# Expert layers of a decoder trunk: slots of 128 tokens with one expert each, or of 32 tokens with four experts each

## The chip, the cores and the metric

The kernel runs on one core of one Trainium2 chip. The metric is the device time of one execution, in microseconds; a lower one is better. The time before is the median of three runs.

## What is computed

One inference step of a two-layer decoder trunk for 512 new prompt tokens and 8 sample tokens, all in float32, model width 1024. The even layer has a convolution and a gated linear attention branch, the odd layer latent attention. Each of the two is followed by an expert layer, and that is what the change touches:

```python
def peer(h, w_q, sub_keys, u_tab, v_tab):   # 8 heads, 16 experts of 16384 per head and token
    q = (xf @ w_q).reshape(n, H_P, 2, D_HALF)
    s = jnp.einsum('nhcd,hckd->nhck', q, sub_keys)
    s_top, i_top = lax.top_k(s, TOPK)
    cand = s_top[:, :, 0, :, None] + s_top[:, :, 1, None, :]
    c_top, c_idx = lax.top_k(cand.reshape(n, H_P, TOPK * TOPK), TOPK)
    ids = i1 * N_KEYS + i2                  # i1, i2: looked up in i_top by c_idx
    gates = jax.nn.softmax(c_top, axis=-1)
    act = jax.nn.gelu(jnp.einsum('td,thkd->thk', xb, u_tab[ids])) * gates
    return jnp.einsum('thk,thkd->td', act, v_tab[ids])
```

For each token and head, 16 experts are chosen. An expert is one row of u and one row of v, 4 KB each. The token's normalised x is dotted with u, the result goes through gelu and is multiplied with the gate, and v is summed with that weight over heads and experts.

## The kernel before, in words

`program` (at the end of the file) runs the even layer, `peer_layer` 0, the odd layer and `peer_layer` 1, each behind a barrier of all engines. Layer 1 also applies the final norm and writes the result.

In `peer_layer` the 512 prompt tokens are four tiles (NT) of 128 tokens, one token per partition. A tile has 8 heads, so there are NW = 32 heads in order, numbered n, and each has 16 **slots**. Slot k of a head is one indirect DMA of POOL (L1096): for each of the 128 tokens, the row of u and v of its k-th expert, 8 KB, into one of RING = 8 buffers `rows`. The 8 sample tokens have 8 slots more, ahead of head 24, in which the 128 partitions already hold 16 picks of each token. A layer has 520 slots.

The order of the work is written out by hand, engine by engine, with semaphores:

- **POOL** issues gather after gather. It waits for `rows_used`, which PE raises when the slot eight places earlier is used up, and at a head's start for its ids (`routed`). For the first head of a layer it waits only for the first 8 ids (`routed_early`).
- **DVE** waits for a landed slot and forms the dot product of all 128 rows with `x_n` (L1414, `dot`). Between the dots it routes the head two places on (AHEAD = 2): `first8`, `next8`, `pairs`, `lookup` and `softmax` at the groups 3 to 7 of a head (a group is two slots). It also normalises the next tile's x (L1280) and adds the finished sum of a tile to x (`add_to_x`, L1423), in one operation of 128x1024.
- **ACT** makes of a slot's 128 dots the weights (`weigh`): gelu (L1178), product with the gate (L1180), and the identity scaled by it, 128x128 (`diag`, L1184). It also copies the queries, their transposes and the scores out of PSUM, computes the exponentials (`exps`, L1170) and the mean squares (`mean_square`, L1121).
- **PE** multiplies the 128x128 `diag` of a slot with its 1024 columns of v, in two matmuls of 512 columns (`experts`, L1581), and sums into one of two accumulators of two PSUM banks over the 128 slots of a tile. At the start of a head stand the `queries` of the head two places on (L1531), behind the first group their transposes (L1545), behind the second the `scores` (L1559). In heads 5, 13 and 21 (TILE_ENDS) the next tile's x is transposed behind the third group (L1508). In heads 16 to 20 the sample's norm, transposes, spread (L1521), queries in column groups of 32 (L1539), scores and routing are done.
- **SP** loads, at a layer's start, the norm's gain, the query weights of 8 heads (1 MB each), the keys (1 MB) and four small constants; in layer 1 also the final norm's gain.

A layer begins with norm, transposes, queries, scores and routing of heads 0 and 1; the first gather follows as soon as head 0's first 8 ids are there.

## Time and profile before

| what | value |
|---|---|
| median of 3 runs | 3477.43 us (3475.92 to 3477.55) |
| the profiled execution's own time, first to last instruction | 3501.1 us |
| PE busy (matmuls) | 2983.7 us, 85% |
| DVE busy | 2185.4 us, 62% |
| ACT busy | 1438.0 us, 41% |
| POOL busy | 1301.9 us, 37% |
| gathered and loaded by POOL's queue | 1128.34 MB, 77.8% of 16 engines' span |
| first and last issue of a gather by ids | 322.7 and 3471.9 us |

A busy time is the time in which an engine had an instruction in work; matmuls are pipelined, so a busy PE is not PE at its peak. The slices are fortieths of the span (87.5 us each). In the timeline a row gives start, duration, engine, line, operation, what is written from what, the form, how many, and in brackets the idle time before and what ended it. The expert layers run from about 300 to 1643 us and from 2150 us to the end.

### The profile page before, as it was taken

The numbers are of one execution on the slowest core, as the hardware profiler recorded it, in microseconds if no ns is written. First come the engines' busy times: TensorE is split into PE (matmuls) and PEld (weight loads), VectorE is DVE, ScalarE is ACT, GpSimd is POOL, SyncE is SP. The second block draws the span as 40 slices with busy tenths as digits, with TensorE's granted clock in tenths as the row PEclk, the third lists the DMA queues.
The fourth block names the chain that finished last, engine by engine and source line by source line (L and its number), as shares of the span: only waits on it lengthen the run. The fifth ranks groups of instructions, "written<-read, shape, count | busy, mean of one in ns | idle before, by whom it ended". The sixth has DMA issues, their size and how long they took to land. (4 is left out here: it accounts for less than half of the span.)

```text
span 3501.1 us, 34014 instructions
## 1 busy us (share of the span) xinstructions
PE 2983.7 (85%) x10561; PEld 1480.5 (42%) x10561; DVE 2185.4 (62%) x5266; ACT 1438.0 (41%) x4182; POOL 1301.9 (37%) x1112
## 2 busy tenths in 40 slices
PE   8987888888889888887999886888888888888886
PEld 7653333433334433333554764434333434433332
DVE  4874667666667766664362334666766676766765
ACT  3122445444444544443351222444444444544444
POOL 0211444444544444452001010445444454444442
PEclk9988999999999999999999897999999999999999
DMA  4015999999999999998203345999999999999998
GB/s 163 29 52 228 421 421 414 421 421 415 420 398 421 418 421 421 421 419 350 81 1 162 134 165 220 421 421 414 421 421 421 415 408 421 409 421 421 421 419 355
DMA packets 178372, 1194.53 MB, mean 341 GB/s; under 512 B 22320, under 2 KB 28240, under 8 KB 38150
## 3 DMA queue, kind: packets, MB, share of 16 engines
q0 software_dynamic: 154368, 1128.34, 77.8%
q1 hardware_dynamic: 22525, 63.11, 4.8%
q8 instruction: 84, 1.38, 0.2%
q10 hardware_dynamic: 1296, 0.90, 0.1%
q14 instruction: 99, 0.80, 0.1%
HBM read 1188.29 MB, written 4.46 MB: 341 GB/s over the span
## 5 line engine op out<-in xcount | busy, mean ns | idle before, releaser
L1581 PE MATMUL p_acc<-p_rows,p_diag 128*128 128x512 f32 (+1 forms) x4160 | 1973.0, 616 | 412.8 <-ACT p_diag L1184 411.0
L1414 DVE CUSTOM_DVE_ANT_0 p_rows<-p_rows,p_x_n 128x1024 f32<-128x1024 f32 x1024 | 1243.7, 1223 | 790.5 <-DMA p_rows<-in_peer_uv,p_ids 788.4
L1096 POOL DMA_INDIRECT p_rows<-in_peer_uv,p_ids x1024 | 1217.0, 1188 | 1384.6 <-PE p_acc L1581 1281.6
L1581 PEld LDWEIGHTS p_acc<-p_rows,p_diag 128*128 128x128 f32 (+1 forms) x4160 | 752.9, 192 | 1508.5 <-ACT p_diag L1184 790.8
L1178 ACT ACTIVATE p_acts<-p_dots 128x1 f32<-128x1 f32 x1040 | 208.3, 200 | 871.8 <-DVE p_dots L1414 870.4
L1184 ACT ACTIVATE p_diag<-ident,p_gated 128x128 f32<-128x128 f32 x1024 | 410.9, 401 | 33.6
L1180 ACT ACTIVATE p_gated<-p_acts,p_gates 128x1 f32<-128x1 f32 x1024 | 301.6, 295 | 33.2
L1531 PE MATMUL p_q_bank<-p_w_q,p_xT 128*128 128x256 f32 x1024 | 234.9, 383 | 2.2 <-ACT p_xT L1127 2.2
L1531 PEld LDWEIGHTS p_q_bank<-p_w_q,p_xT 128*128 128x128 f32 x1024 | 196.1, 192 | 55.5 <-issue 28.5
L1150 ACT COPY p_q_rows<-p_q_bank 128x256 f32<-128x256 f32 x68 | 25.2, 370 | 347.7 <-PE p_q_bank L1531 347.7
L1623 POOL DMA_INDIRECT smp_past<-in_cache_rows,smp_row_ids x32 | 30.0, 937 | 361.1 <-PE c_ps L2096 227.4
L1178 ACT ACT_TABLE_LOAD x73 | 93.7, 1283 | 8.7 <-DVE p_dots L1414 7.5
L2469 PE MATMUL d_turn<-ident,smp_past 128*128 128x128 f32 x512 | 78.0, 311 | 15.6 <-DVE d_kpeT L2353 14.4
L541 DVE SCALAR_TENSOR_TENSOR a_conv<-a_u,a_conv_wc,a_conv 128x512 f32<-128x512 f32 x120 | 86.6, 792 | 0.0
L688 PE MATMUL a_ps<-a_xT,a_w_in 128*128 128x260 f32 x384 | 85.7, 384 | 0.1
L1414 DVE DVE_READ_ACCUMULATOR2_ANT p_dots<- 128x1 f32 x1040 | 85.1, 82 | 0.0
L1170 ACT ACT_TABLE_LOAD x64 | 82.1, 1283 | 1.1
L688 PEld LDWEIGHTS a_ps<-a_xT,a_w_in 128*128 128x128 f32 x384 | 72.5, 190 | 11.9 <-issue 0.4
L2469 PEld LDWEIGHTS d_turn<-ident,smp_past 128*128 128x128 f32 x512 | 68.8, 162 | 19.9 <-DVE d_kpeT L2353 16.3
L2359 DVE COPY d_ckvT<-d_turn 128x512 f32<-128x512 f32 x64 | 42.1, 687 | 56.2 <-PE d_turn L2469 56.1
L2294 ACT COPY d_ckvT<-d_turn 128x512 f32<-128x512 f32 x64 | 34.7, 587 | 103.0 <-PE d_turn L2469 103.0
L1088 POOL MEMSET p_eps<- 128x1 f32 x2 | 0.2, 98 | 171.2 <-POOLq L62 171.2
(402 smaller groups left out, 2483.0 us busy)
## 6 DMA issues: line engine op xcount, KB each, us to landing
p_w_q<-in_w_q_heads SPq DMA_DIRECT2D x16, 1024.0 KB, 12.2
p_rows<-in_peer_uv,p_ids POOLq DMA_INDIRECT x1024
a_w_in<-in_ab_w_in SPq DMA_DIRECT2D x6, 1024.0 KB
a_w_in<-in_ab_w_out SPq DMA_DIRECT2D x1, 4096.0 KB
c_arena<-in_c_w_out SPq DMA_DIRECT2D x1, 4096.0 KB, 12.7
smp_past<-in_c_w_out SPq DMA_DIRECT2D x1, 4096.0 KB
a_w_in<-in_ab_w_in SPq DMA_DIRECT2D x4, 1008.0 KB, 21.3
smp_past<-in_w_qx SPq DMA_DIRECT2D x1, 3072.0 KB, 18.6
```

What stands on the lines that cost most here:

```text
L541: ins = nc.vector.scalar_tensor_tensor(out=conv[:, c, 0:SEQ], in0=u[:, c, i:i + SEQ], scalar=conv_wc[:, c, i:i + 1], in1=conv[:, c, 0:SEQ] ...
L688: last = nc.tensor.matmul(ps[bank][:, 512 * b:512 * b + half], w_in[:, k, at:at + 128], xT[:, k, half_of(b)], start=(k == 0), stop=(k == K ...
L1096: nc.gpsimd.indirect_dma_start(out=rows[:, slot % RING, :], out_offset=None, in_=w[f"peer_uv{layer}"], in_offset=bass.IndirectOffsetOnAxis ...
L1170: nc.scalar.activation(ex[:], rel[:], ACT.Exp, accum_out=ex_sum[:]).then_inc(ex_ready, 1)
L1178: nc.scalar.activation(acts[:, i % 4, j:j + 1], dots[:, i % 4, j:j + 1], ACT.Gelu).then_inc(gelud, 1)
L1180: nc.scalar.mul(gated[:, i % 4, j:j + 1], acts[:, i % 4, j:j + 1], gate[:, j:j + 1]).then_inc(gated_ready, 1)
L1184: nc.scalar.mul(diag[:, i % 4, j, 0:n], unit[:], gated[:, i % 4, j:j + 1]).then_inc(diag_ready, 1)
L1414: nc.vector.tensor_tensor_reduce(rows[:, k % RING, 0:D_MODEL], rows[:, k % RING, 0:D_MODEL], x, 1.0, 0.0, ALU.mult, ALU.add, dots[:, slot ...
L1531: last = nc.tensor.matmul(q_bank[:, 0:D_KEY], xT[:, k, :], w_q[:, h, k, :], start=(k == 0), stop=(k == KC - 1))
L1581: last = nc.tensor.matmul(acc[done % 2][0:n, at], diag[:, slot // GROUP % 4, j, 0:n], rows[:, (slot + j) % RING, D_MODEL + 512 * b:D_MODEL ...
L2359: nc.vector.tensor_copy(buf(g)[:, half, :], bank(0, half)).then_inc(turn_dve, 1)
L2469: last = nc.tensor.transpose(turn[i % 2][:, KEYS * c + 128 * a:KEYS * c + 128 * a + 128], latent(b, NQ * g + a, c), ident[:])
```

## The change

A slot now holds four experts of each of 32 tokens, for the same 128 tokens and experts in all. The tile's tokens are four quarters q ("quads"), and the 16 slots of a head are four for each q. On partition 32 e + p of a slot sits token 32 q + p with its experts of index e modulo 4.

- ids and gates are computed as before, with a token per partition, into `pick`. Then PE moves them into the new arrangement with 16 small matmuls (`spread_picks`, 32 identity columns and 8 columns of data each), and DVE copies them from PSUM into `ids` and `gates`, in two operations. POOL and ACT wait for that (`picked`). In the loop it stands behind the first group on PE and the third on DVE, for the head after the present one.
- x is repeated four times: for each q, two matmuls of 512 columns (`spread_x`) write the 32 tokens' rows into all four quarters of the partitions, and ACT copies them out (`x_rep_out`, 128x1024). For the first tile this stands among the steps of the start, for the others in the last head of the tile before. DVE's dots use this copy.
- the weights are 128x32 (32 identity columns) in place of 128x128. The sum runs in four column groups: 256 of the 1024 columns each, into 32 partitions each of one of four accumulators (one per q, a half bank each), which take two banks in all.
- adding the sum to x is now 8 operations of 32x256 for two of the quarters, twice a tile; for the sample 4 of 8x256.
- the first head's early ids are gone: the first gather waits for all of them and for the moved picks.
- one more constant of 64 KB is loaded; in layer 1 the final gain is loaded later, into the buffer of the norm's gain, once all norms are done. PSUM for transposes is shared in one counted order of turns.

```diff
...
-                if n == 0:
-                    pool.wait_ge(routed_early, 1)
-                else:
-                    pool.wait_ge(routed, route_no(n) + 1)
+                pool.wait_ge(picked, n + 1)
...
+            def x_rep_out(t, q):
+
+                act.wait_ge(turn_ps, rep_turn(t, q) + 1)
+                if t:
+                    act.wait_ge(dotted, first_slot(H_P * t - 1) + QUADS * (q + 1))
+                nc.scalar.copy(x_rep[:, q, :], turn[:, :]).then_inc(turn_used, 1)
...
-                    nc.scalar.mul(diag[:, i % 4, j, 0:n], unit[:], gated[:, i % 4, j:j + 1]).then_inc(diag_ready, 1)
+                    nc.scalar.mul(weights[:, i % 4, j, 0:n], unit, gated[:, i % 4, j:j + 1]).then_inc(weights_ready, 1)
...
             s_out(0)
+            x_rep_out(0, 0)
+            x_rep_out(0, 1)
             q_out(1)
             qT_out(1, qT[:])
+            x_rep_out(0, 2)
             exps(0)
             s_out(1)
+            x_rep_out(0, 3)
             exps(1)
...
+            def spread_picks(m):
+
+                dve.wait_ge(pick_ps, m + 1)
+                nc.vector.tensor_copy(ids[:, m % (AHEAD + 1), :].rearrange("p (q j) -> p q j", q=QUADS), by_quad[:, :, 0, :])
+                nc.vector.tensor_copy(gates[:, m % (AHEAD + 1), :].rearrange("p (q j) -> p q j", q=QUADS), by_quad[:, :, 1, :]).then_inc(picked, 1)
...
+            def add_to_x(t, bank):
+
+                for q in (2 * bank, 2 * bank + 1):
+                    dve.wait_ge(rows_used, first_slot(H_P * t + H_P - 1) + QUADS * (2 * bank + 2))
+                    for c in range(PARTS):
+                        at = x_sb[quad(q), t, part(c)]
+                        last = nc.vector.tensor_tensor(at, at, acc[quad(c), q, :], ALU.add)
+                last.then_inc(acc_used, 1)
...
+            def spread_x(t, q):
+
+                if t == 0 and q == 0:
+                    pe.wait_ge(small_in, 80)
+                pe.wait_ge(turn_used, rep_turn(t, q))
+                for b in range(2):
+                    at = slice(512 * b, 512 * b + 512)
+                    last = nc.tensor.matmul(turn[:, at], quads[quad(q), :], x_n[quad(q), at], start=True, stop=True)
+                last.then_inc(turn_ps, 1)
...
+            def spread_picks(m):
+
+                pe.wait_ge(routed, route_no(m) + 1)
+                pe.wait_ge(gates_ready, route_no(m) + 1)
+                if m:
+                    pe.wait_ge(picked, m)
+                for q in range(QUADS):
+                    for e in range(4):
+                        last = nc.tensor.matmul(by_quad[quad(e), q], ident[:, quad(q)], pick[:, :, e:TOPK:4], start=True, stop=True)
+                last.then_inc(pick_ps, 1)
...
-                    pe.wait_ge(diag_ready, slot + j + 1)
-                    for b in range(2):
-                        at = slice(512 * b, 512 * b + 512)
-                        last = nc.tensor.matmul(acc[done % 2][0:n, at], diag[:, slot // GROUP % 4, j, 0:n], rows[:, (slot + j) % RING, D_MODEL + 512 * b:D_MODEL + 512 * b + 512],
+                    pe.wait_ge(weights_ready, slot + j + 1)
+                    for c in range(PARTS):
+                        at = D_MODEL + D_PART * c
+                        last = nc.tensor.matmul(dst[QUAD * c:QUAD * c + n], weights[:, slot // GROUP % 4, j, 0:n], rows[:, (slot + j) % RING, at:at + D_PART],
                                                 start=(first and j == 0), stop=(end and j == GROUP - 1))
                     last.then_inc(rows_used, 1)
...
                 scores(m)
+                spread_x(0, 2 * m)
+                spread_x(0, 2 * m + 1)
+            spread_picks(0)
+            spread_picks(1)
...
+                    if g % 2 and h == H_P - 1 and t < NT - 1:
+                        spread_x(t + 1, q)
```

## Rows read from the trace of the kernel before

**Rows 1.** The page: GB/s moved by the DMA engines in 40 equal slices.

```profile
GB/s 163 29 52 228 421 421 414 421 421 415 420 398 421 418 421 421 421 419 350 81 1 162 134 165 220 421 421 414 421 421 421 415 408 421 409 421 421 421 419 355
```

**Rows 2.** Waits of POOL: for whom; us in total, times, longest us.

```profile
POOL p_rows L1096 <- PE p_acc L1581: 1302.9, 903, 10.4
```

**Rows 3.** Groups by line: busy us, mean ns of one; idle before, releasers.

```profile
L1581 PE MATMUL p_acc<-p_rows,p_diag 128*128 128x512 f32 (+1 forms) x4160 | 1973.0, 616 | 412.8 <-ACT p_diag L1184 411.0
L1414 DVE CUSTOM_DVE_ANT_0 p_rows<-p_rows,p_x_n 128x1024 f32<-128x1024 f32 x1024 | 1243.7, 1223 | 790.5 <-DMA p_rows<-in_peer_uv,p_ids 788.4
...
L1178 ACT ACTIVATE p_acts<-p_dots 128x1 f32<-128x1 f32 x1040 | 208.3, 200 | 871.8 <-DVE p_dots L1414 870.4
L1184 ACT ACTIVATE p_diag<-ident,p_gated 128x128 f32<-128x128 f32 x1024 | 410.9, 401 | 33.6
L1180 ACT ACTIVATE p_gated<-p_acts,p_gates 128x1 f32<-128x1 f32 x1024 | 301.6, 295 | 33.2
...
L1309 DVE TENSOR_TENSOR p_cand<-p_top 128x256 f32<-128x256 f32 x66 | 27.6, 419 | 0.0
```

**Rows 4.** Windows of 40 us: busy by engine, then granted clock, DMA share, GB/s.

```profile
410.00:450.00 40.00, 33.10 (x86) 14.94 (x84) 26.84 (x66) 17.58 (x54) 18.66 (x17) 1.00 1.01 421
530.00:570.00 40.00, 34.96 (x94) 16.99 (x94) 28.34 (x71) 22.17 (x61) 20.26 (x17) 0.96 0.99 406
970.00:1010.00 40.00, 35.25 (x90) 16.67 (x88) 27.56 (x66) 19.94 (x60) 17.28 (x15) 0.87 0.93 369
2820.00:2860.00 40.00, 34.14 (x93) 16.27 (x93) 29.07 (x71) 21.21 (x63) 21.63 (x16) 0.96 0.96 393
```

**Rows 5.** Windows at the start of layer 0, columns as in rows 4.

```profile
300.00:324.00 24.00, 15.28 (x64) 12.21 (x65) 8.57 (x38) 6.78 (x12) 1.42 (x2) 0.79 0.97 385
312.00:316.00 4.00, 2.98 (x16) 2.19 (x16) 0.00 (x0) 0.74 (x2) 0.00 (x0) 1.00 1.01 424
```

**Rows 6.** Timeline of the start of layer 0.

```profile
315.37 0.68 PE L1559 MATMUL p_s_bank<-p_keysT,p_qT 128*128 128x128 f32 x4 [0.55 <-ACT p_qT L1154]
315.89 3.62 PE L1531 MATMUL p_q_bank<-p_w_q,p_xT 128*128 128x256 f32 x16
...
319.37 0.43 DVE L1313 MAX8 p_best<-p_cand 128x8 f32<-128x256 f32 x1
...
320.96 0.68 PE L1559 MATMUL p_s_bank<-p_keysT,p_qT 128*128 128x128 f32 x4 [0.56 <-ACT p_qT L1154]
...
322.68 1.14 POOL L1096 DMA_INDIRECT p_rows<-in_peer_uv,p_ids  x1 [22.41 <-DVE p_ids L1343]
```

**Rows 7.** Timeline: the sample's spread of x and its queries in column groups.

```profile
1035.23 1.98 PE L1521 MATMUL p_turn<-p_x_smp,p_spread 8*128 8x512 f32 x4
...
1037.25 1.01 ACT L1146 COPY p_x_smp<-p_turn 128x1024 f32<-128x1024 f32 x1 [0.28 <-PE p_turn L1521]
...
1075.61 3.66 PE L1539 MATMUL p_q_bank<-p_w_q,p_xT_smp 128*32 128x256 f32 x64
1079.20 6.28 PE L1581 MATMUL p_acc<-p_rows,p_diag 128*128 128x512 f32 x14
```

**Rows 8.** Chain of waits at the start of layer 1: start us, us, what.

```profile
2149.97 4.19 DMA p_gain<-in_ffn_norm
```

**Rows 9.** Timeline, POOL and PE, at the starts of heads 3, 5 and 16 of layer 0.

```profile
458.58 3.70 PE L1581 MATMUL p_acc<-p_rows,p_diag 128*128 128x512 f32 x8 [1.33 <-ACT p_diag L1184]
...
460.83 0.94 POOL L1096 DMA_INDIRECT p_rows<-in_peer_uv,p_ids  x1 [5.11 <-PE p_acc L1581]
...
540.27 5.40 PE L1581 MATMUL p_acc<-p_rows,p_diag 128*128 128x512 f32 x8 [2.74 <-ACT p_diag L1184]
...
544.14 1.83 POOL L1096 DMA_INDIRECT p_rows<-in_peer_uv,p_ids  x1 [8.12 <-PE p_acc L1581]
...
985.04 5.46 PE L1581 MATMUL p_acc<-p_rows,p_diag 128*128 128x512 f32 x6 [2.83 <-ACT p_diag L1184]
```

**Rows 10.** Timeline behind the last gather of layer 1.

```profile
3491.60 1.22 DVE L1423 TENSOR_TENSOR x_sb<-x_sb,p_acc 128x1024 f32<-128x1024 f32 x1 [1.89 <-PE p_acc L1581]
```

More of the change, by code:

```diff
@@ L1141, in smp_xT_out @@
                         at = DEC_BATCH * u + 16 * twin
-                        nc.scalar.copy(xT_smp[:, u, :, at:at + DEC_BATCH], src).then_inc(smp_xT, 1)
+                        nc.scalar.copy(xT_smp[:, u, :, at:at + DEC_BATCH], src).then_inc(turn_used if u and twin else smp_xT, 1)
             def smp_spread_out():
-                act.wait_ge(smp_spread, 1)
-                nc.scalar.copy(x_smp[:], turn[:, :]).then_inc(smp_full, 1)
+                act.wait_ge(turn_ps, SMP_REP_TURN + 1)
+                nc.scalar.copy(x_smp[:], turn[:, :]).then_inc(turn_used, 1)
             def q_out(i):
@@ L1490, in _ @@
                         if g == 6 + late:
-                            lookup(route_no(m), ids[:, m % (AHEAD + 1), :])
+                            lookup(route_no(m), pick[:, 0, :], m)
                 if m < NW:
-                    softmax(route_no(m), gates[:, m % (AHEAD + 1), :])
-            add_to_x(4, NT - 1)
+                    softmax(route_no(m), pick[:, 1, :])
+            add_to_x(NT - 1, 1)
             if out:
@@ L1534, in smp_queries @@
             def smp_queries(u):
-                pe.wait_ge(smp_xT, 4)
+                pe.wait_ge(smp_xT, 3)
+                pe.wait_ge(turn_used, SMP_X_TURN + 1)
                 pe.wait_ge(qT_ready, smp_query_no(u))
+                for j in range(4):
+                    pe.wait_ge(w_q_in[4 * u + j], 16)
                 for k in range(KC):
```

211 lines of the change are left out of this document (104 added, 107 removed).

## The prediction

> **What bounds the kernel now.** First the page's slices: in both expert stages the DMA engines move 414 to 421 GB/s nearly throughout, and the few lower slices (408, 409, 398) are what a change there could win back [rows 1]. A gather brings 128 rows of 8 KB, 1.0486 MB, so at 421 GB/s a slot takes 2.49 us, and 1040 slots take 2590 us of the span of 3501.1. Then the waits: POOL waits 1302.9 us for PE, since a slot of the ring must be free [rows 2], and DVE's idle time before its dots, 788.4 us, ends with a landed gather [rows 3]. Both belong to one loop: eight slots go round gather, dot, gelu and weights, expert matmuls. Which part limits it is read from the groups: per slot, DVE needs 1.22 us, ACT 0.90 (0.20 + 0.30 + 0.40), and PE four instructions (4160 for 1040 slots) whose starts lie some 0.44 us apart, as eight take 3.70 and one 0.6, so some 1.75 us [rows 3, 9]; each is under 2.49. PE looks 85% busy, yet the DMA engines are what is full. The windows confirm it: a common 40 us stretch moves 421 GB/s at DMA share 1.01, and only a few move less: 406, 369, 393 [rows 4].
>
> So the matmuls that the change makes cheaper are covered by the gathers. The time can move in three places only: where the DMA engines run dry, before the first gather of a layer, and behind the last one.
>
> **The gathers themselves: 0.** A slot still has 128 rows of 8 KB, and there are still 1040. Plain weight loads run at much the same rate (424 in the window 312 to 316, before any gather [rows 5]), so it is the engines that limit, not which rows are asked for. The 512 KB for the final gain move from the start of layer 1 into its gathers, where they cost 1.2 us that the start saves.
>
> **The expert matmuls: off the path.** A slot becomes four column groups of 256 columns, eight instructions (each float32 call shows as two). The nearest row is the sample's queries, 128x32 weights and 256 columns in four groups: 64 in 3.66 us, 0.057 us each [rows 7]; eight are 0.46 us, where 1.75 stood. If groups did not overlap, 16 query matmuls in 3.62 us (0.226 each) give 1.8 us, no change [rows 6]. I take 0.5. Of ACT's weights, 0.40 goes towards 0.30; hidden too.
>
> Switching between whole-width and 32-column matmuls costs nothing visible: those 64 begin at 1075.61, take 3.66 and are followed by expert matmuls at 1079.20 [rows 7], no gap.
>
> **The start of a layer: the large term.** Before, the first gather is issued at 322.68, once half the ids are known [rows 6]. After, it needs all 16, the gates too, PE's spreading of both, and DVE's copy. ACT and PE also get the four repeats of x ahead of it. Step by step in layer 0, from the end of head 0's scores at 315.37 + 0.68 = 316.05: first repeat 1.98 (as the sample's spread) and its copy 1.01 [rows 7], second repeat 1.98 to 321.02; queries of head 1, 3.62, to 324.64; then from their end to the end of head 1's scores as before (319.51 to 321.64, 2.13) to 326.77 [rows 6]; third repeat 1.98 and copy 1.01 to 329.76; only then ACT's exponentials, with a table load 1.28 + 0.4, to 331.45; gates 0.5 to 331.95; 32 small matmuls at 0.057, 1.8, to 333.8; two small copies 0.4: 334.2. The Trainium skill ("TensorEngine Tiling (Array Packing)", Instruction Overhead) gives each matmul some 60 cycles of overhead and no more for few columns. By that rule, as an estimate, 32 of them take 32 x 60 cycles at 2.4 GHz = 0.8 us, and the sum at the end would be 2 us lower; no row here is that small a matmul, so I keep the nearest row's 1.8.
>
> DVE's own routing does not set the end: from its row at 319.37 [rows 6] it has eleven operations left, and even at twice 0.42 us each [rows 3] that ends at 328.6. It is the repeats ahead of the exponentials on PE and ACT that set the end. Issue is late by 11.5 us.
>
> What covers this is the load of weights. To 324 the engines had moved 385 x 24 = 9.24 MB [rows 5] of the 9.96 MB asked for before the gathers (0.52 + nine times 1.05); they run dry at 325.7. From issue to first byte no row tells directly; a 0.52 MB load took 4.19 us to landing [rows 8], 1.24 of them data, so launch and finish make 2.9; I take 2.0. Data begin at 336.2, the engines idle for 10.5 us; the twin in layer 1 makes it **+21**. Bounds: launch 0 to 3.8 (with POOL's 0.94), the small matmuls half or double: 7.5 to 14 a layer, 15 to 28 for both. Slot 8 is not late: eight gathers keep the engines fed for 20 us, to 356, and DVE's second routing (twenty-odd operations, some 9 us from 334.2), spread, first gelu and matmul end by about 351.
>
> **Where the engines ran dry.** Against 421, a stretch of 406 lacks 40 x 15/421 = 1.4 us, 369 lacks 4.9, 393 lacks 2.7 [rows 4]; one more like the last (394) lacks 2.6, three like the first (406, 405, 409) 4.0; the smaller ones 2.4: 18 us in all. They lie behind heads in which ACT does a norm and waits for queries. In a common head POOL waits 5.11 us and nothing is lost; behind a norm 8.12 us [rows 9], and PE starts at half clock there: eight instructions in 5.40 us and six in 5.46, where eight take 3.70. After: PE finishes the last two slots in 1 instead of 3.7 us, so queries begin 2.5 earlier, and the first slot frees some 3 us earlier. That would give back nearly all 18. Against it, at the turn of each tile ACT copies four repeats (1.01 each), the last one waiting for PE (1.98) between last slot and next queries: 3 to 4 us, about what was won, with more at half clock. I take **-12** (bounds -16 and, with starving turns, +4).
>
> **Inside the heads: 0.** DVE gets two small copies a head and sixteen adds of 32x256 a tile (by the 0.42 us of a 128x256 operation [rows 3], 6.7 us in place of 1.22), with 1.2 us spare per slot. PE's 32 small matmuls stand behind the head's first two slots; behind them wait transposed queries and ACT's copy, some 2 us of slack I do not see used up; DVE asks for them six slots into the head, 15 us. POOL needs the ids only ten slots later. Cover gone, 60 heads at even 0.3 us would be 18 us; it is in the upper range.
>
> **Behind the last gather.** The last slot's matmuls go from 1.9 to about 0.7 us, but eight adds stand in place of one of 1.22 us [rows 10]: 8 x 0.33 to 0.42 = 2.6 to 3.4. Net +0.3 in layer 0; in layer 1 DVE also has eight adds (2.6 to 3.4 us) inside the last head, whose final scalings leave it nearly no slack: +1.5. Together **+2** (0 to 4).
>
> **Sum:** 21 - 12 + 2 = +11. The profiled span is 3501.1, which would become 3512; the median of the runs is 3477.4, 24 us less, so I add the same 11 there: **3488 us**. Some 7 us (0.2%) is about what a measurement can tell.
>
> **Rivals.**
> 1. PE turns cold (3505, chance 0.20). With 0.5 us of work in 2.49, PE idles 2 us per slot. After 2.74 us idle, eight instructions took 5.40 us, and after 2.83 six took 5.46, where eight take 3.70 [rows 9]: half clock, 1.2 GHz. Queries would take up to 7.2 us and repeats 4.0; a tile's turn is then 16 to 18 us after its last dot where about 12 can be borne, 4 to 6 us lost at two turns a layer, 20 in all, and 2 in small dips, where 18 were lost: +4 in place of -12, so 21 + 2 + 4. For it: 2.74 us were enough. Against: 1.33 us of idle left the 3.70 untouched, and 2 us lies between. The Trainium skill ("TensorE: Matmul & The Clock Gate", HAM oscillation) says that idle gaps between bursts bring the clock back to half rate again and again. [...]
> 2. Groups don't overlap (3500, 0.07). The change does not do what it says, PE stays at 1.75 us plus new work, nothing comes back: 21 + 2. Against it stands the 0.057 us of [rows 7].
> 3. Start shorter and all stalls gone (3480, 0.15): 17 - 15 + 1 = +3, within the noise.
> 4. Faster (3470, 0.08): slots free 1.3 us earlier in each round, so more gathers queue. If that lifted 421 to 424, the rate of one window in [rows 5], 2590 x 0.7% = 18 us come off: 11 - 18 = -7. It decides from 422 on. Against: at share 1.01 the queue is full already.
> My forecast has the other 0.50.
>
> **Range.** 3478 to 3508: the unknowns of the start (15 to 28) and of the stalls (-16 to +4) partly cancel; it takes in rivals 1 to 3 and leaves out most of 4. **Chances:** faster by over 0.2%: 0.08; same: rival 3 and the low end of the forecast, 0.22; slower: 0.70.
>
> **What would show it.** First gather of layer 0 about 334 instead of 322.7, with an empty stretch of some 10 us on the DMA engines before it, in both layers: if absent, the main term is wrong. Expert matmuls 8 per slot in about 0.5 us; granted clock around the queries (1.0 or 0.5) decides between forecast and rival 1; windows of 406 and 369 back at 421, or new dips at heads 8, 16 and 24 of a layer. A common window at 424 would make rival 4 right.

## The result, and the profile after

The kernel after takes 3521.33 us (median of 4 runs, 3519.58 to 3524.04), the kernel before 3477.17 (4 runs, 3475.92 to 3477.55) on the same chip: a ratio of 1.0125 [1.0111, 1.0139], 44 us slower. The forecast was 3488 and the range ended at 3508: the direction was right, and the size was short by a factor of four.

The page after, engine line, granted clock and DMA rate in the same 40 slices as [rows 1]:

```profile
PE 2223.4 (63%) x16897; PEld 1048.8 (30%) x16897; DVE 2236.6 (64%) x5506; ACT 1380.7 (39%) x4214; POOL 1231.2 (35%) x1112
...
PEclk9988666666667666665999997666666667666665
...
GB/s 162 25 55 156 422 420 421 395 421 421 421 390 421 421 421 409 421 421 356 144 1 162 94 249 177 422 421 421 398 421 421 420 389 420 421 421 413 421 421 345
```

The full slices are as before, so a gather costs what it did. Lower are the slice in which each layer starts (228 to 156, 220 to 177) and three slices a layer (395, 390, 409, and 398, 389, 413). The granted clock lies near 0.65 in both expert layers, where it was near 1.0.

The groups by line that answer to [rows 3], and the adds and repeats:

```profile
L1626 PE MATMUL p_acc<-p_rows,p_weights 128*32 128x256 f32 x8192 | 940.1, 551 | 1172.3 <-ACT p_weights L1217 1157.4
L1217 ACT ACTIVATE p_weights<-p_quads,p_gated 128x32 f32<-128x32 f32 x1024 | 329.0, 321 | 33.5
L1541 PE MATMUL p_turn<-p_x_n,p_quads 32*128 32x512 f32 x128 | 101.7, 935 | 4.4 <-ACT p_x_rep L1160 4.4
L1439 DVE TENSOR_TENSOR x_sb<-x_sb,p_acc 32x256 f32<-32x256 f32 x128 | 53.4, 417 | 4.7 <-PE p_acc L1626 3.1
```

The matmuls did what the change meant: 940 us of PE work where 1973 stood. PE now waits 1157 us for weights, and nothing came of it.

**Three lengths locate the loss.** Each expert layer can be cut at four marks of the timeline: the load of the gain that opens it, its first gather, its last gather, and the first load of what follows (or the end of the span). Here they are for the kernel after, both layers:

```profile
301.43 0.36 SPq L1095 DMA_DIRECT2D p_gain<-in_ffn_norm  x1
...
1643.56 0.94 POOL L1127 DMA_INDIRECT p_rows<-in_peer_uv,p_ids  x1 [1.55 <-PE p_acc L1626]
...
1667.68 0.38 SPq L1773 DMA_DIRECT2D c_arena<-in_c_w_in  x1
...
2145.88 0.34 SPq L1095 DMA_DIRECT2D p_gain<-in_ffn_norm  x1
...
2185.05 0.94 POOL L1127 DMA_INDIRECT p_rows<-in_peer_uv,p_ids  x1 [38.57 <-DVE p_gates L1397]
...
3487.86 0.94 POOL L1127 DMA_INDIRECT p_rows<-in_peer_uv,p_ids  x1 [1.54 <-PE p_acc L1626]
```

With the first gather of layer 0 at 340.44 (next rows), layer 0 has a **start** of 39.0 us, a **middle** of 1303.1 and an **end** of 24.1, layer 1 has 39.2, 1302.8 and (to 3521.1) 33.2. The same cuts in every profile of this study, each as the sum of both layers:

| kernel | start | middle | end | both layers |
|---|---|---|---|---|
| before | 45.7 | 2597.6 | 51.2 | 2694.5 |
| before, second chip (e0) | 45.9 | 2597.3 | 51.2 | 2694.3 |
| **after** | **78.2** | **2605.9** | **57.4** | **2741.5** |
| after, another chip (a0) | 77.7 | 2607.0 | 57.4 | 2742.1 |
| e1 column groups alone | 48.0 | 2593.4 | 51.0 | 2692.4 |
| e2 picks first | 53.3 | 2608.7 | 57.3 | 2719.3 |
| e3 PE kept busy | 77.2 | 2629.9 | 58.3 | 2765.4 |
| e4 quarter of the adds | 79.5 | 2597.8 | 50.2 | 2727.5 |
| e6 adds later | 77.0 | 2595.1 | 59.2 | 2731.3 |
| e7 picks handed over sooner | 79.8 | 2607.6 | 57.3 | 2744.6 |
| e8 last repeat later | 77.6 | 2593.9 | 57.4 | 2728.9 |
| e9 repeats from all rows | 67.1 | 2598.7 | 57.3 | 2723.0 |
| e10 e2, e6 and e8 | 54.4 | 2595.4 | 59.1 | 2708.9 |
| e11 and weights first | 55.0 | 2593.4 | 59.2 | 2707.6 |
| e12 all moves | 54.9 | 2593.5 | 56.2 | 2704.7 |
| e13 before, weights first | 47.7 | 2595.9 | 51.1 | 2694.7 |

So the change costs 32.5 us at the starts, 8.4 in the middles and 6.2 at the ends: 47. Two kernels that share a start in their text can differ in it by some 2 us: layer 1 of e4 and e7 starts in 41.1 us, that of a0 and e6 in 38.7, though neither edit touches it. Start and middle also overlap. In before the weights are still being loaded when the first gather is issued, and the DMA engines are never empty there (share 1.00 to 1.02 in every window of 4 us from 320 to 340). In after they are empty for 14.6 us in layer 0 (windows from 324 to 348) and 14.8 in layer 1 (2168 to 2192), 29.4 together. The other 3 us of the 32.5 are load of weights that has moved out of the middle, so the stalls inside the middles grew by some 11 us and not by 8.4. A count as in the prediction says the same: over thirty-one windows of 40 us in each layer, from 10 us behind the first gather on, the rate falls short of 421 GB/s by 16.9 us of transfers in before and by 27.9 in after.

The layer between the two expert layers, which it leaves alone, takes 506.9 us in the profile of before and 478.2 in that of after; that is why the two spans differ by only 20 us, and why the sums above are compared and not the spans.

**The start of layer 0**, timeline, where [rows 6] had the first gather at 322.68:

```profile
317.87 1.98 PE L1541 MATMUL p_turn<-p_x_n,p_quads 32*128 32x512 f32 x4
...
320.95 3.78 PE L1541 MATMUL p_turn<-p_x_n,p_quads 32*128 32x512 f32 x4 [1.10 <-ACT p_x_rep L1160]
...
324.65 6.65 PE L1564 MATMUL p_q_bank<-p_w_q,p_xT 128*128 128x256 f32 x16
...
333.37 1.98 PE L1541 MATMUL p_turn<-p_x_n,p_quads 32*128 32x512 f32 x4
...
335.38 1.01 ACT L1160 COPY p_x_rep<-p_turn 128x1024 f32<-128x1024 f32 x1 [2.77 <-PE p_turn L1541]
336.41 1.28 ACT L1203 ACT_TABLE_LOAD   x1
...
339.21 0.62 PE L1617 MATMUL p_pick_bank<-p_pick,ident 128*32 128x8 f32 x32
...
340.44 1.14 POOL L1127 DMA_INDIRECT p_rows<-in_peer_uv,p_ids  x1 [38.45 <-DVE p_gates L1397]
```

The chain is the one that the prediction wrote down, down to ACT's exponentials behind the copy of the third repeat; but the second repeat and the queries run at half clock, 3.78 and 6.65 us for the 1.98 and 3.62 that were put in. What it does to the DMA engines, in windows as in [rows 5], and below them a common stretch and the first tile turn, as in [rows 4]:

```profile
320.00:324.00 4.00, 3.05 (x4) 1.16 (x4) 3.86 (x20) 0.89 (x1) 0.00 (x0) 0.55 1.01 416
...
328.00:332.00 4.00, 3.54 (x12) 2.53 (x10) 0.00 (x0) 0.37 (x1) 0.00 (x0) 0.67 0.04 16
332.00:336.00 4.00, 2.79 (x10) 1.18 (x8) 0.00 (x0) 0.99 (x2) 0.00 (x0) 1.00 0.00 0
336.00:340.00 4.00, 3.38 (x36) 1.29 (x36) 0.50 (x4) 2.92 (x6) 0.00 (x0) 0.68 0.00 0
340.00:344.00 4.00, 0.00 (x0) 0.00 (x0) 3.96 (x25) 0.33 (x1) 2.95 (x3) 0.50 0.41 125
...
410.00:450.00 40.00, 21.23 (x182) 8.60 (x182) 27.43 (x70) 16.70 (x57) 18.71 (x17) 0.63 1.01 420
...
650.00:690.00 40.00, 29.68 (x182) 12.04 (x184) 32.22 (x82) 18.25 (x57) 15.53 (x12) 0.60 0.90 368
```

Of the windows from 328 to 340 two are empty and one nearly so. The dips of [rows 4] (behind heads with a norm) are gone, and new ones stand where a tile turns, at heads 8, 16 and 24 of each layer: 368 here, then 398, 399, 368, 354 and 409 (the second of them cuts its dip in two; 975 to 1015 has 354).

**A tile turn**, timeline of PE, DVE, ACT and POOL around the first dots of head 8:

```profile
657.24 3.41 DVE L1439 TENSOR_TENSOR x_sb<-x_sb,p_acc 32x256 f32<-32x256 f32 x8
...
667.10 1.43 POOL L1127 DMA_INDIRECT p_rows<-in_peer_uv,p_ids  x1 [6.50 <-PE p_acc L1626]
...
672.34 1.22 DVE L1428 CUSTOM_DVE_ANT_0 p_rows<-p_rows,p_x_rep 128x1024 f32<-128x1024 f32 x1
...
673.44 3.78 PE L1541 MATMUL p_turn<-p_x_n,p_quads 32*128 32x512 f32 x4
...
677.15 6.19 PE L1564 MATMUL p_q_bank<-p_w_q,p_xT 128*128 128x256 f32 x16
...
683.38 0.37 ACT L1183 COPY p_q_rows<-p_q_bank 128x256 f32<-128x256 f32 x1 [5.11 <-PE p_q_bank L1564]
...
684.68 1.32 PE L1626 MATMUL p_acc<-p_rows,p_weights 128*32 128x256 f32 x16 [1.34 <-ACT p_weights L1217]
...
685.61 0.94 POOL L1127 DMA_INDIRECT p_rows<-in_peer_uv,p_ids  x1 [9.12 <-PE p_acc L1626]
```

Two delays fall close together. The eight small adds stand in the middle of DVE's routing, and POOL waits 6.50 us; then head 8's first pair of dots is done by 673.6, but ACT makes their weights only behind the copy of the queries, which wait on PE behind the last repeat: 673.44 to 683.34 for these two at half clock. No slot comes free until 685, and POOL waits 9.12.

### The profile page after: what moved, and what is told of

Same layout as the page of the kernel before. It is cut to its first block and busy times, and to the rows that moved or that the text cites. A ratio compares the mean times of both kernels' runs of the same rounds, so it can differ in the third digit from the quotient of the medians.

```text
span 3521.1 us, 47144 instructions
## 1 busy us (share of the span) xinstructions
PE 2223.4 (63%) x16897; PEld 1048.8 (30%) x16897; DVE 2236.6 (64%) x5506; ACT 1380.7 (39%) x4214; POOL 1231.2 (35%) x1112
## 5 line engine op out<-in xcount | busy, mean ns | idle before, releaser
L1428 DVE CUSTOM_DVE_ANT_0 p_rows<-p_rows,p_x_rep 128x1024 f32<-128x1024 f32 x1024 | 1242.2, 1223 | 754.7 <-DMA p_rows<-in_peer_uv,p_ids 754.5
L1626 PE MATMUL p_acc<-p_rows,p_weights 128*32 128x256 f32 x8192 | 940.1, 551 | 1172.3 <-ACT p_weights L1217 1157.4
L1127 POOL DMA_INDIRECT p_rows<-in_peer_uv,p_ids x1024 | 1146.8, 1120 | 1488.2 <-PE p_acc L1626 1273.0
L1626 PEld LDWEIGHTS p_acc<-p_rows,p_weights 128*32 128x32 f32 x8192 | 197.0, 129 | 1855.9 <-ACT p_weights L1217 1798.2
L1217 ACT ACTIVATE p_weights<-p_quads,p_gated 128x32 f32<-128x32 f32 x1024 | 329.0, 321 | 33.5
L1564 PE MATMUL p_q_bank<-p_w_q,p_xT 128*128 128x256 f32 x1024 | 334.5, 497 | 2.2 <-ACT p_xT L1153 2.2
L1213 ACT ACTIVATE p_gated<-p_acts,p_gates 128x1 f32<-128x1 f32 x1024 | 301.6, 295 | 33.2
L1564 PEld LDWEIGHTS p_q_bank<-p_w_q,p_xT 128*128 128x128 f32 x1024 | 259.2, 261 | 104.7 <-issue 52.0
L1541 PE MATMUL p_turn<-p_x_n,p_quads 32*128 32x512 f32 x128 | 101.7, 935 | 4.4 <-ACT p_x_rep L1160 4.4
L688 PEld LDWEIGHTS a_ps<-a_xT,a_w_in 128*128 128x128 f32 x384 | 72.5, 190 | 11.9 <-issue 0.4
L2524 PE MATMUL d_turn<-ident,smp_past 128*128 128x128 f32 x512 | 67.1, 284 | 0.6 <-DVE d_kpeT L2408 0.3
L2524 PEld LDWEIGHTS d_turn<-ident,smp_past 128*128 128x128 f32 x512 | 59.2, 145 | 2.9 <-DVE d_kpeT L2408 1.8
```

The lines of the kernel that those rows point to most:

```text
L688: last = nc.tensor.matmul(ps[bank][:, 512 * b:512 * b + half], w_in[:, k, at:at + 128], xT[:, k, half_of(b)], start=(k == 0), stop=(k == K ...
L1127: nc.gpsimd.indirect_dma_start(out=rows[:, slot % RING, :], out_offset=None, in_=w[f"peer_uv{layer}"], in_offset=bass.IndirectOffsetOnAxis ...
L1213: nc.scalar.mul(gated[:, i % 4, j:j + 1], acts[:, i % 4, j:j + 1], gate[:, j:j + 1]).then_inc(gated_ready, 1)
L1217: nc.scalar.mul(weights[:, i % 4, j, 0:n], unit, gated[:, i % 4, j:j + 1]).then_inc(weights_ready, 1)
L1428: nc.vector.tensor_tensor_reduce(rows[:, k % RING, 0:D_MODEL], rows[:, k % RING, 0:D_MODEL], x, 1.0, 0.0, ALU.mult, ALU.add, dots[:, slot ...
L1541: last = nc.tensor.matmul(turn[:, at], quads[quad(q), :], x_n[quad(q), at], start=True, stop=True)
```

## The experiments

Fourteen runs, two of them of kernels that are not changed, in four groups; those of one group ran on one chip, with before beside them.

**e0, before again.** No edit.

> The kernel before, unchanged, for a second profile. Its first profile had a span of 3501.1 us beside a median of 3477, and the odd layer in it took 506.9 us where the changed kernel's profile has 478.2, though nothing there was changed. If the surplus of 24 us belongs to that one execution, this profile spans about 3476 and its odd layer takes about 480 us; if profiling lengthens this kernel always, about 3501 and 507 again. Time: 3477, ratio 1.000.

3504.67 us, 0.9998 [0.9989, 1.0008]. Both expert layers take 2694.3 us, as in the profile of before to 0.2 us. On this chip and the next ones before takes 3502 to 3506 instead of 3477. The layer in between takes 503 to 510 us in their profiles, whichever kernel it is, as in the first profile of before (506.9), and 478 only in that of after. So that difference does not come from the change; whether it is the chip or the time at which it ran, no run tells.

**e1, the column groups alone.** In the kernel before, the expert matmuls take weights of 32 columns and write four column groups; the adds then take one group's columns (what is added to x is therefore wrong, and the adds are one operation still, not the eight of after).

```diff
-                    for b in range(2):
-                        last = nc.tensor.matmul(acc[done % 2][0:n, at], diag[..., 0:n], rows[..., 512 * b ...])
+                    for c in range(4):
+                        last = nc.tensor.matmul(acc[done % 2][32 * c:32 * c + m, 0:256], diag[..., 0:m], rows[..., 256 * c ...])
```

> The kernel before with the expert matmuls alone in four column groups of 32 columns of weights and 256 of data; the slots, the start, ids and adds stay as before (the sums are then not the right ones: a slot's 128 tokens share 32 output rows). Theory A, PE with little work falls to half clock: mean granted clock about 0.70 instead of 0.965, queries about 6.4 us instead of 3.6, and since neither start nor tile turns have anything added, the time stays within 3470 to 3488. Theory B, the half clock comes from something else in the change (small matmuls, waits for copies): clock 0.95 or more, stalls of the gathers nearly gone, 3477 - 15 = 3462.

3503.62 us, 0.9997 [0.9987, 1.0006]. Its expert matmuls, from the groups, and those of e3 (below), kept at full clock:

```profile
L1582 PE MATMUL p_acc<-p_rows,p_diag 128*32 128x256 f32 x8320 | 975.4, 557 | 1263.5 <-ACT p_diag L1184 1193.5
```

```profile
L1631 PE MATMUL p_acc_smp<-p_w_q,ident 128*128 128x256 f32 x5952 | 1557.9, 398 | 0.0
...
L1627 PE MATMUL p_acc<-p_rows,p_weights 128*32 128x256 f32 x8192 | 669.9, 399 | 180.8 <-ACT p_weights L1218 176.4
```

The mean granted clock falls from 0.964 to 0.702 by this edit alone, and the time does not move: neither do the cheap matmuls win much (3.9 us in the middles, of which the starts take 2.1), nor does the half clock cost anything while PE has slack. What e1 has does not cost time. What it lacks is the new work and the new order of the rows in the slots.

**e2, picks first.** In after, head 0's exponentials, gates and picks go ahead of all repeats; the last two repeats go into head 0.

```diff
                 scores(m)
-                spread_x(0, 2 * m)
-                spread_x(0, 2 * m + 1)
             spread_picks(0)
+            spread_x(0, 0)
+            spread_x(0, 1)
             spread_picks(1)
```

> The changed kernel with another start: exponentials, gates and the moving of the picks of head 0 before any repeat of x; repeats 0 and 1 behind them, 2 and 3 inside head 0. If the repeats ahead of the exponentials set the start: first gather about 26 to 27 us behind a layer's first load instead of 39, the empty stretch of 15 us shrinks to 3, and two layers save 24 us: 3521 - 24 = 3497 (ratio 1.006). If the start is hidden by something else, or the repeats then hold up the first slots by as much: above 3512.

3529.45 us, 1.0067 [1.0050, 1.0084]. The first gathers come 26.9 and 26.4 us into the layers for 39, and the starts fall by 25 us to 53.3; the ends stay, and the middles are 2.8 longer (2608.7), for which no run gives a reason. The order of work at the start is the largest single cost of the change, as the prediction had it. What is left over before's 45.7 is the hand-over by PE and the wait for the gates.

**e3, PE kept busy.** Three needless 128x128x256 matmuls (two instructions each) behind the expert matmuls of each prompt slot.

```diff
+                    for k in range(WARM if warm else 0):
+                        nc.tensor.matmul(acc_smp[:, 0:256], ident[:], w_q[:, 0, k, :], start=True, stop=True)
```

> The changed kernel with three needless matmuls (128x128 weights, 256 columns, result unused) behind each prompt slot's expert matmuls except in head 24, some 1.3 us of PE work per slot at full clock. Theory A, the half clock causes the deeper stalls at the tile turns: clock about 0.95, queries 3.6 us, the stalls (27.5 us of lost gathers by windows) fall by 12 to 18 us, 3521 - 15 = 3506; the start keeps its cold part. Theory B, the added adds and copies cause the stalls and the clock only goes with them: clock 0.95 too, but the time within 5 us of 3521 or above it.

3578.52 us, 1.0211 [1.0193, 1.0228], slower than after by far. Theory A fell, and theory B had room for it ("or above it") without a reason for so much. PE works 3260 us of 3574, and the middles are 24 us longer; most likely the needless work itself (1558 us) delays slots in heads with queries, which was not tested. It is a bad way to ask what the half clock costs; it says only that a stretch of 40 us at the first turn (660 to 700) still moves 368 GB/s at clock 1.00. e9 asked better. It leaves the starts as they were (77.2), since no needless matmul stood there.

**a0, after again**, on the chip of e4, e6 and e7. No edit.

> The kernel after, unchanged, as the level for the three that share its chip. The pair of e0 and before on the last chip gave spans some 27 us longer than the chip of the first comparison, all of it in the odd layer that the change leaves alone. If the cost is fixed in us (theory), after stands 44 us above before here too: 1.0125 plus or minus 0.001. If it scales with something of the chip, the ratio is off by more than that.

3555.33 us, 1.0144 [1.0127, 1.0161]. In us it is 49 above before, where the first comparison had 44; the intervals of the two ratios overlap, and in the profile the expert layers together are as on the first chip to 0.6 us (their middles differ by 1.1).

**e4, a quarter of the adds** (only the first column part is added to x, three quarters of the prompt's expert sum left out).

```diff
-                    for c in range(PARTS):
+                    for c in range(1):
```

> The kernel after with only one of the four column parts added to the tokens (2 adds of 32x256 where 8 were, so 0.85 us where 3.4 us were, at 14 places; three quarters of the prompt's expert sum is left out of the output). Theory A, the adds that stand ahead of the routing at a tile turn make the new stalls of heads 8, 16 and 24: stalls fall from 14 to about 8 us a layer, the ends of the layers give 2.5 us each, together 1.0125 -> 1.008. Theory B, the stalls come from ids that are handed over late (after the third pair of dots of a head): stalls stay at 13 to 14, only the ends gain: 1.011.

3539.14 us, 1.0092 [1.0075, 1.0109]. Middles 2607.0 to 2597.8, ends 57.4 to 50.2: the adds are worth 9.2 us in the middles, more than the 8.4 by which the lengths grew, and more than all of the loss at the ends. The ratio alone lies between the two theories (1.008 and 1.011); it is the middles that speak for A.

**e6, the adds later.** The first half of a tile's adds goes behind the softmax of its last head, the second behind the next head's copy of the picks. Same output.

```diff
-                    if g == 5 and n % H_P == H_P - 1:
-                        add_to_x(t, 0)
...
                     softmax(route_no(m), pick[:, 1, :])
+                if n % H_P == H_P - 1:
+                    add_to_x(t, 0)
```

> The kernel after with both add calls moved: the first from inside the routing of a tile's last head to behind its softmax, the second from before the hand-over of the picks to behind it. Same work, same output. Theory A: the routing and the ids of head 9, 17 and 25 come 3.4 us sooner each, stalls fall by 3 to 5 us a layer: about 1.010. Theory B (hand-over late anyway): within 1 us a layer for head n, 1.012. Against both: the dots of the next tile wait behind the adds instead, and the rows of the ring come free 3.4 us later: 1.0125 or above.

3542.95 us, 1.0110 [1.0093, 1.0126], against a0's 1.0144. The interval holds both theories; the lengths decide. The middles fall by 11.9 us, below those of before, with all the adds still made. So it was their place that cost, as long as the repeat and the queries behind them stay as they are. The ends rise by 1.8, since both halves now stand in series at the end of the last head. The timeline of its turn:

```profile
662.44 0.94 POOL L1127 DMA_INDIRECT p_rows<-in_peer_uv,p_ids  x1 [3.78 <-PE p_acc L1626]
...
665.80 3.41 DVE L1439 TENSOR_TENSOR x_sb<-x_sb,p_acc 32x256 f32<-32x256 f32 x8
...
679.20 0.94 POOL L1127 DMA_INDIRECT p_rows<-in_peer_uv,p_ids  x1 [9.46 <-PE p_acc L1626]
```

The adds now start at 665.80, when the routing is done. POOL's first wait is 3.78 us for 6.50; its second one is about as long as in after (9.46 for 9.12). One of the two can be borne, both cannot.

**e7, picks handed over sooner.** PE spreads a head's picks ahead of the queries, and DVE copies them behind the first pair of dots.

```diff
+                if 0 < n < NW - 1:
+                    spread_picks(n + 1)
                 if m < NW:
                     queries(m)
```

> The kernel after with the hand-over of the picks sooner: the 32 small matmuls stand ahead of a head's queries on PE, and DVE copies them behind the first pair of dots instead of the third, some 5 us sooner in each head. Same output. Theory B, late ids empty the DMA queue: stalls fall from 14 to 8 us a layer or below: 1.009. Theory A (the adds): stalls fall by 3 at most, 1.0115. If DVE must wait for PE there, which stands behind the experts of the head before, every head loses up to 1 us and the ratio goes above 1.0125.

3553.06 us, 1.0128 [1.0112, 1.0145], no difference from a0 that the intervals allow, and the middles are the same to 0.6 us (the 2.1 us more in the starts are all in that of layer 1, which the edit leaves alone). Late ids were a theory that fell: the hand-over inside the heads costs nothing.

**e8, the last repeat later.** The fourth repeat of the next tile goes behind the first experts of that tile's first head.

```diff
-                    if g % 2 and h == H_P - 1 and t < NT - 1:
+                    if g in (1, 3, 5) and h == H_P - 1 and t < NT - 1:
                         spread_x(t + 1, q)
+                    if g == 0 and h == 0 and t:
+                        spread_x(t, 3)
```

> The kernel after with one move alone: the fourth repeat of the next tile goes from behind the last experts of a tile to behind the first experts of the next, and its copy behind the copy of the queries. In the trace of e6 the last repeat (3.78 us) and the queries (5.18 us), both at half clock, stood in series on PE ahead of the first weights of head 8, whose dots were long done, and POOL waited 9.46 us for a free slot. Theory C, this chain makes the stalls that the moved adds left: three turns a layer by 3.8 us less chain, stalls 15 -> 9 to 11 a layer, ratio 0.0025 to 0.004 below after (1.0144 or 1.0125, by the chip). Rival (the adds alone make them, the queue holds the chain): unchanged within 0.001.

3539.31 us, 1.0104 [1.0088, 1.0119]. The timeline of its turn:

```profile
667.28 1.43 POOL L1127 DMA_INDIRECT p_rows<-in_peer_uv,p_ids  x1 [6.49 <-PE p_acc L1626]
...
673.63 4.54 PE L1564 MATMUL p_q_bank<-p_w_q,p_xT 128*128 128x256 f32 x16
...
680.44 0.94 POOL L1127 DMA_INDIRECT p_rows<-in_peer_uv,p_ids  x1 [3.79 <-PE p_acc L1626]
```

The mirror of e6: the first wait stays (6.49), the queries start with no repeat ahead of them, the second wait falls from 9.12 to 3.79, and the middles are again near the lowest of this study (2593.9).

**e9, repeats from all rows.** The repeats multiply all 128 rows of x by a matrix that is zero for the rows that do not belong. Same columns, same output. The matrix (`quad_rows`) is zeroed and loaded at the layer's start besides; the first repeat starts at 317.89 us for 317.87.

```diff
-                    last = nc.tensor.matmul(turn[:, at], quads[quad(q), :], x_n[quad(q), at], start=True, stop=True)
+                    last = nc.tensor.matmul(turn[:, at], quad_rows[:, q, :], x_n[:, at], start=True, stop=True)
```

> The kernel after with the repeats read from all 128 rows (a matrix with zeros for the rows that don't belong) instead of 32; same columns, same output. The clock fell at the first repeats of the start in every trace in which they stand there, and did not where queries stood in their place. Theory D, PE counts for the clock by how much of it works: the start stays at full clock, the second repeat takes 1.98 us for 3.78, the queries 3.62 for 5.2 to 6.65, the first gather comes 4 to 5 us sooner (34 to 35 us after the layer's first load for 39), and the ratio falls by 0.0025. Rival, the clock falls by the pauses between short pieces of work: first gather at 39, no change.

3528.64 us, 1.0069 [1.0055, 1.0082], where a0 had 1.0144. Timeline of the start of layer 0:

```profile
317.89 1.88 PE L1546 MATMUL p_turn<-p_x_n,p_quad_rows 128*128 128x512 f32 x4
...
320.88 1.98 PE L1546 MATMUL p_turn<-p_x_n,p_quad_rows 128*128 128x512 f32 x4 [1.10 <-ACT p_x_rep L1165]
322.70 3.62 PE L1569 MATMUL p_q_bank<-p_w_q,p_xT 128*128 128x256 f32 x16
...
334.50 1.15 POOL L1132 DMA_INDIRECT p_rows<-in_peer_uv,p_ids  x1 [32.05 <-DVE p_gates L1402]
```

Same instructions at the same places, all at full clock, and the first gather at 33.1 us into the layer; the prediction had put it at 34.5 (334.2 less 299.71). The starts fall by 10.6 us against a0, and the DMA engines are empty for 16.5 us in both together (8.0 and 8.5), where after had 29.4. At the turn the queries take 3.62 us and POOL's second wait is 5.88, and the middles fall by 8.3. The one edit takes back 19 us of the two layers. So the half clock of those few instructions made more than a third of the loss (with the adds and the place of the last repeat left as they were), while the same half clock in e1 cost nothing.

**e10, e11, e12: the moves together.** e10 has e2, e6 and e8. e11 lets ACT make a head's first pair of weights ahead of its copy of the queries. e12 adds e9's repeats and, in a layer's last head, puts the first adds behind the fifth pair of dots.

```diff
-                if m < NW:
-                    q_out(query_no(m))
                 act.wait_ge(picked, n + 1)
...
                 gelu(i)
+                if m < NW:
+                    q_out(query_no(m))
                 gelu(i + 1)
...
+                    if g == 4 and n == NW - 1:
+                        add_to_x(t, 0)
```

> The three moves together on the kernel after: picks ahead of the repeats (e2, -0.0058), adds out of the routing (e6, -0.0034) and the last repeat later (e8, -0.003 expected). If they add up: 1.0144 - 0.0122 = 1.002, first gather at 26.5 us, stalls 5 to 7 us a layer, ends of layers 2 to 3 us each still above before. If they share a cause: 1.005.

> As e10, and in every head ACT makes the first pair of weights ahead of the copy of the queries, so that the queries (5.2 us at half clock) no longer stand ahead of the first freed slots. If the queries at half clock are what is left of the stalls: 3 to 5 us a layer less than e10, level with before (1.000). If the queue holds them: as e10.

> e11 (1.003) with the repeats read from all 128 rows, and in a layer's last head the first adds stand behind the fifth pair of dots, where DVE waits for rows, and no longer in one piece of 6.9 us with the last ones at the end. If the kernel after lost its time by the clock at the start (3.4 to 5.7 us of empty DMA left in e10 and e11), by the adds, the last repeat and the ends, and by nothing else: start 1 to 3 us a layer, ends 3.4 us a layer sooner, 1.0000 plus or minus 0.0015. If column groups or the four-expert slots cost the transfers something by themselves: it stays at 1.002 or above with stalls below those of before.

3514.05 us, 1.0036 [1.0022, 1.0050]; 3513.65, 1.0030 [1.0017, 1.0042]; 3512.74, 1.0030 [1.0019, 1.0041]. The moves do not add up to 1.002, since e6 and e8 win the same 12 us; e11's order changes nothing that the intervals can tell. e12 was expected level with before and is not. Its middles are 4 us shorter than before's, its ends 5.0 longer and its starts 9.2 longer, and that is its 10 us. In the windows it falls short of 421 GB/s by 9.1 us where before does by 16.9, so by its letter the other theory of the expectation holds (above 1.002 with fewer stalls). A small cost of the new slots to the transfers is therefore not excluded, but e13 below shows the same pattern in the slots of before: fewer stalls and no time won. The timeline of its start shows why e9's repeats do not help there:

```profile
327.67 0.62 PE L1626 MATMUL p_pick_bank<-p_pick,ident 128*32 128x8 f32 x32 [3.44 <-DVE p_pick L1398]
328.22 3.76 PE L1550 MATMUL p_turn<-p_x_n,p_quad_rows 128*128 128x512 f32 x4
...
328.89 1.14 POOL L1132 DMA_INDIRECT p_rows<-in_peer_uv,p_ids  x1 [26.04 <-DVE p_gates L1404]
```

With the picks first, the clock is at half behind PE's 3.44 us of idle, but nothing that the first gather needs is behind it. What is left is the hand-over: all ids and the gates, PE and two copies, where before half the ids were enough.

**e13, before with the weights first**, e11's order in the kernel before.

```diff
-                if m < NW:
-                    q_out(query_no(m))
                 act.wait_ge(gates_ready, route_no(n) + 1)
                 gelu(i)
+                if m < NW:
+                    q_out(query_no(m))
                 gelu(i + 1)
```

> The kernel before with one order changed: ACT makes the first pair of weights of a head ahead of the copy of its queries. Against e11, to see whether the smaller stalls there (4 to 5.7 us a layer, 9 in before) come from the slots of four experts or from this order. If from the order: stalls of before 9 -> 6 us a layer, ratio 0.998. If from the order of experts in the slots: unchanged, 1.0000 within 0.0007.

3501.98 us, 0.9998 [0.9989, 1.0007]: nothing to win in the order of ACT. Yet the order does to the dips what the expectation's first theory said. These are the windows in which before had 406, 369 and 393 GB/s [rows 4], now in e13:

```profile
530.00:570.00 40.00, 34.56 (x95) 16.06 (x94) 28.76 (x71) 23.06 (x62) 19.38 (x16) 1.00 1.01 421
970.00:1010.00 40.00, 34.78 (x93) 15.66 (x92) 29.19 (x68) 22.04 (x63) 19.82 (x16) 0.97 1.01 410
...
2820.00:2860.00 40.00, 34.97 (x94) 16.06 (x93) 28.98 (x71) 21.68 (x65) 17.92 (x16) 0.97 1.01 421
```

By the prediction's count these three lacked 9 us of transfers, and they lack 1 now, but the middles are only 1.7 us shorter. Other windows are lower instead: 1070 to 1110 has 413 for 420, 1150 to 1190 has 412 for 421. Why, the record doesn't show. A dip that is filled is thus not time that is won. No kernel of this study beats before by more than its interval.

## Why the prediction was wrong

**The gathers, 0: right.** 420 to 422 GB/s in full slices, as before.

**The expert matmuls, off the path: right, but taken at half the size they have at half clock.** The weights took 0.32 us for the 0.3 expected. Eight matmuls take 1.08 us at half clock and 0.64 at full (e8, at 687.38, clock 1.00), for the 0.5 taken. e1 shows that neither matters.

**The start, +21: the step that failed most.** The forecast had the first gather later by 11.5 us a layer and, of these, the DMA engines empty for 10.5, hence 21. Measured are 16.0 and 16.4 us later (the +32.5 of the table) and 29.4 us of empty engines. The steps and their order held; the durations were all put in at full clock, from rows taken there. e9, which keeps that clock, has its first gathers 10.1 and 11.2 us later than before's and 16.5 us of empty engines: with the clock as assumed, the forecast was even a little high. Of layer 0's missing 4.5 us, 1.8 are in the second repeat, 3.0 in the queries, and 0.6 in the fourth repeat, which at half clock still ran when the gates were ready, so that the picks waited for it; the small matmuls gave 1.2 back, 0.62 us for 1.8. The half clock was in the text as rival 1, with "queries up to 7.2 us, repeats 4.0", but only its cost at the turns was priced; its own price for the start stayed at 21. What misled was the reasoning by idle time alone (2.74 us of idle enough, 1.33 not): here PE was idle for 1.10 us and worked before and behind it, and the clock fell all the same. For the 32 small matmuls the Trainium skill ("TensorEngine Tiling (Array Packing)", Instruction Overhead) gave an estimate of 0.8 against the 1.8 taken, and the trace's 0.62 is nearer to it.

**The stalls, -12: wrong in sign, +8.4 by the lengths and some +11 without their overlap.** Two steps failed. First, what could be won: 18 us of shortfall were read from windows, and the forecast took them for time that faster matmuls give back. The dips did go, as forecast: after has 421 GB/s from 530 to 570, where before had 406. But among all kernels here, with and without the cheap matmuls, no sum of middles is below 2593.4, against before's 2597.6, and e13 fills 8 of the 9 us that the three windows of [rows 4] lacked, for 1.7 us of middle. Some 4 us are the most that any run got; the 18 were no stock. (Every kernel here with the cheap matmuls, e3 with its needless work aside, runs its common heads near half clock, so what they would give at full clock without other work stays open.) Second, the turn: the prediction counted the last repeat and the queries (3 to 4 us, "more at half clock") but put the sixteen adds under "inside the heads: 0", as a total of 6.7 us a tile against a slack per slot. They do not come spread: eight of them, 3.41 us, stand at once in the middle of a routing chain, one wait ahead of the repeat and the queries. e6 and e8 show that either delay alone is carried by the eight slots, and both are not. e9 shows the part of the clock in it: with the adds where they were, but the repeat and the queries at 6.3 us together for 9.9, the middles are 8.3 us shorter.

**Inside the heads, 0: right for the picks** (e7), wrong for the adds, as said.

**The ends, +2: +6.2, the same mechanism mis-sized.** Eight adds took 3.45 us, just above the 2.6 to 3.4, for the 1.22 of the one before, and the last slot's matmuls 1.1 at half clock for the 0.7 taken. The end of layer 0 is 2.2 us longer where 0.3 net was taken. In layer 1 it is 4.0 for 1.5, most likely by the 3.42 us of adds inside the last head. e4, with a quarter of the adds, has both ends below those of before.

**The sum.** 32.5 + 8.4 + 6.2 = 47 us in the expert layers of the two profiles (or 29.4 + 11 + 6.2, in the prediction's own terms), for the 11 forecast; the medians say 44 on one chip and 49 on another. All three terms missed the same way; only the direction was right.

**The rivals.** Rival 1, PE turns cold, was the right mechanism with too small a price: it should have had its 8 us more in the start (29 + 4 + 2 = 35, or 3512). PE is idle for some 1.4 us between two slots, and a common window has a granted clock of 0.63; where PE has slack that rate cost nothing (e1). The Trainium skill ("TensorE: Matmul & The Clock Gate", HAM oscillation) describes the half rate coming back again and again in waits between bursts. The waits of its example are longer than the 1.4 us here, so the trace shows that rate where the example alone would not have led one to expect it, and the trace decides. Rival 2 fell: groups do overlap. Rival 3 rested on stalls that were not there to win, and rival 4 on a faster rate, which no full window shows (420 to 422).

## What to carry to other kernels

Here cheaper work on an engine that was not the bound won nothing and turned its clock down. So price every serial chain on such an engine, at starts and turns, at half clock; that chain, not the engine's total, is where it cost. Ask of each new piece of work where it stands, not only how much it is: eight adds of 3.4 us in the middle of a routing chain, with the last repeat and the queries close behind, cost some 12 us of transfers in two layers, and next to nothing once either had been moved. And before counting dips in the transfer rate as recoverable, run one kernel that takes the suspected cause away, and see how much shorter the middle really gets.

## What the runs showed of the hardware

- Four matmul instructions of 512 columns that read 32 rows (1.98 us) were followed, after 1.10 us of idle, by half clock (3.78 us for the next four in layer 0, where the window 320 to 324 has 0.55, and 3.10 in layer 1); the same four from 128 rows (1.88 us), with the same pause, by full clock (1.98 us in both layers). With what it did at the turns the edit was worth 19 us (e9).
- A kernel can run at a mean granted clock of 0.70 instead of 0.96 at no cost in time (e1).
- A DVE add of 32x256 takes 0.42 us, and eight of them 3.41 to 3.45 us, where one of 128x1024, twice the numbers of those eight, takes 1.22.
- The 32 small matmuls of 8 columns in four column groups took 0.62 us together at the start of layer 0, 0.019 us each, and 0.46 at a turn.
- The kernel before takes 3477 us on one chip and 3502 to 3506 on four others. The profiles place a difference of that size in the layer between (478.2 us in the profile of after, 503 to 510 in all others); the expert layers of one kernel agree between chips to 0.6 us in sum.
